# Up projection of a decoder layer: the low halves of three right operands are computed on GpSimd at the change of span

## The reference, cut to what matters

```python
h = rmsnorm(x, norm_ffn_pre[l])
up = causal_depthwise_conv(h @ w_up[l], conv_w[l], conv_b[l])   # w_up: 1024 x 5632
gate, val = up[..., :D_FF], up[..., D_FF:]                       # D_FF = 2816
f = (jax.nn.silu(gate) * val) @ w_down[l]
x = x + rmsnorm(f, norm_ffn_post[l])

def causal_depthwise_conv(h, conv_w, conv_b):                    # CONV_WIDTH = 3
    S = h.shape[1]
    hp = jnp.pad(h, ((0, 0), (CONV_WIDTH - 1, 0), (0, 0)))
    y = conv_b
    for kk in range(CONV_WIDTH):
        y = y + conv_w[kk] * hp[:, kk:kk + S]
    return y
```

## Time and profile before

| | us |
|---|---|
| median of 3 runs | 2625.34 (2622.07 to 2629.64) |
| the profiled execution: its own time | 2622.72 |
| its span in the trace | 2621.0 |
| PE busy in the span | 2432.5 (93%) |
| DVE busy in the span | 1653.4 (63%) |
| POOL busy in the span | 737.3 (28%) |
| the up projection in the span | about 1214 to 2092 |
| the stretch of the change of span | about 1640 to 1692 |

### The profile page before, as it was taken

One profiled execution on the slowest core, in us unless ns is written; L12 is line 12 of the kernel. 1 busy time (PEld: TensorE's weight loads), 2 busy tenths in 40 slices (PEclk: granted clock), 3 DMA queues, 4 the chain that ended last, 5 costly groups with the idle time before them and its releaser, 6 DMA issues. The chain is left out here.

```text
span 2621.0 us, 38066 instructions
## 1 busy us (share of the span) xinstructions
PE 2432.5 (93%) x11925; PEld 2000.5 (76%) x11925; DVE 1653.4 (63%) x2099; ACT 1230.4 (47%) x2065; POOL 737.3 (28%) x624
## 2 busy tenths in 40 slices
PE   6989996999999979994999999799999899999997
PEld 5767885878788868883888888688888778778785
DVE  4424222999898977874877777877777734443433
ACT  4311112888888864554444444444444423242322
POOL 0000001686666643554222222222222000110101
PEclk9989997999999989996999999899999999999999
DMA  7922435243333215676232222523222154545452
GB/s 240 286 65 80 132 122 148 57 123 91 86 89 86 73 54 162 217 241 192 73 94 74 86 82 76 181 72 96 72 88 80 65 188 145 188 148 192 148 189 107
DMA packets 283122, 326.90 MB, mean 125 GB/s; under 512 B 11972, under 2 KB 217468, under 8 KB 278396
## 3 DMA queue, kind: packets, MB, share of 16 engines
q1 hardware_dynamic: 278396, 308.68, 38.5%
q0 software_dynamic: 4608, 16.78, 1.6%
HBM read 216.36 MB, written 92.27 MB: 118 GB/s over the span
## 5 line engine op out<-in xcount | busy, mean ns | idle before, releaser
L740 POOL TENSOR_TENSOR weight<-beta,stick 128x512 f32<-128x512 f32 (+3 forms) x320 | 304.4, 958 | 601.8 <-ACT beta L694 449.9
L786 DVE TENSOR_TENSOR_SCAN stick<-z_ps,stick,beta 128x512 f32<-128x512 f32 x192 | 245.2, 1277 | 25.2 <-ACT z_ps L695 24.2
L511 PE MATMUL out_ps<-hT,w_hi 128*128 128x512 f32 x768 | 240.4, 395 | 9.8 <-DVE w_lo L445 9.8
L1629 PE MATMUL value_chain_ps<-wide,wu_hi 128*128 128x512 f32 x704 | 220.2, 394 | 16.4 <-DVE up_cols L1578 9.7
L694 ACT ACTIVATE beta<-z_ps 128x512 f32<-128x512 f32 (+3 forms) x320 | 170.7, 533 | 92.1 <-PE z_ps L820 78.5
L1409 ACT ACTIVATE wu_hi<-wu_sums 128x512 fp32r<-128x512 f32 x175 | 110.4, 632 | 187.3 <-PE value_chain_ps L1629 93.0
L837 PE MATMUL wT_ps<-ident,weight 128*128 128x128 f32 x1088 | 174.0, 275 | 11.0 <-POOL weight L740 11.0
L1746 POOL TENSOR_TENSOR y<-y,x 128x1024 f32<-128x1024 f32 x16 | 38.9, 2432 | 504.8 <-DVE y L1805 504.6
L511 PEld LDWEIGHTS out_ps<-hT,w_hi 128*128 128x128 f32 x768 | 145.5, 190 | 42.2 <-DVE w_lo L445 10.2
L695 ACT ACTIVATE z_ps<-z_ps 128x512 f32<-128x512 f32 (+3 forms) x320 | 171.5, 536 | 0.0
L1629 PEld LDWEIGHTS value_chain_ps<-wide,wu_hi 128*128 128x128 f32 x704 | 134.0, 191 | 45.6 <-DVE wu_lo L1506 10.0
(11 more groups left out here) (209 smaller groups left out, 6232.2 us busy)
## 6 DMA issues: line engine op xcount, KB each, us to landing
wu_f<-in_w_down SPq DMA_DIRECT2D x88, 512.0 KB, 3.5
wu_f<-in_w_up SPq DMA_DIRECT2D x44, 512.0 KB, 5.0
bridge<-in_w_up SPq DMA_DIRECT2D x44, 512.0 KB, 5.0
f_scratch<-f SPq DMA_DIRECT2D x44, 512.0 KB, 2.6
wu_sums<-f_scratch SPq DMA_DIRECT2D x88, 256.0 KB, 3.7
x_scratch<-x SPq DMA_DIRECT2D x56, 256.0 KB, 2.6
xt<-in_x SPq DMA_DIRECT2D x16, 512.0 KB, 5.7
hT<-h_hi SPq DMA_DIRECT2D x16, 512.0 KB, 4.7
```

What stands on the lines that cost most here:

```text
L511: m = pe.matmul(out_ps[half + j][:, :], w[slot][:, k, :], hT[h][:, k, j * BANK:(j + 1) * BANK], start=(k == 0 and t == 0), stop=(k == kc - ...
L740: pool.tensor_tensor(weight[v % weight_ring][:, 0:w], beta[v % stick_in][:, 0:w], stick[q % 2][:, at:at + w], ALU.mult).then_inc(weight_do ...
L786: dve.tensor_tensor_scan(stick[q % 2][:, at:at + w][:, ::-1], backwards, beta[u % stick_in][:, 0:w], start, ALU.mult, ALU.bypass).then_inc ...
L1629: m = pe.matmul(bank[:, :], w[left][:, k, :], x[right][:, k, :], start=(not adds and k == 0 and t == 0), stop=(k == half - 1 and t == 2), ...
```

## The change

At the change of span, the low halves of right operands 2, 4 and 6 are computed on GpSimd (`by_pool`), those of 0, 1, 3 and 5 still on VectorE. In the first span nothing is changed. The three have a semaphore of their own, `x_pool_done`, and TensorE's wait in `ready` looks at the one or the other.

```diff
+        x_pool_done = n.sem("x_pool_done")
+        by_pool = (2, 4, 6)
@@ GpSimd
+                def right_low(part, operand):
+                    pool.wait_ge(x_hi_done, 7 * part + operand)
+                    pool.tensor_tensor(x_lo[operand], as_f32(x_lo[operand]), as_f32(x_hi[operand]), ALU.subtract).then_inc(x_pool_done, 1)
+
                 def unit(u, part, j, e, pair):
                     if not is_last(u):
                         left_sums(u + 1, 1 - e, pair + e)
+                    if at_part_end(u, part):
+                        right_low(part + 1, 2)
+                        right_low(part + 1, 4)
+                    if past_part_end(u, part):
+                        right_low(part, 6)
@@ VectorE
                 def right_low(part, operand):
+                    if part > 0 and operand in by_pool:
+                        return
                     dve.wait_ge(x_hi_done, 7 * part + operand)
@@ TensorE
                 def ready(u, operand, part):
                     i = UP_LEFT.index(operand)
                     pe.wait_ge(wu_done, split_of(u, operand))
-                    pe.wait_ge(x_done, 7 * part + i + 1)
+                    if part == 0:
+                        pe.wait_ge(x_done, i + 1)
+                    elif i in by_pool:
+                        pe.wait_ge(x_pool_done, len(by_pool) * (part - 1) + by_pool.index(i) + 1)
+                    else:
+                        pe.wait_ge(x_done, 7 + (7 - len(by_pool)) * (part - 1) + sum(1 for k in range(i + 1) if k not in by_pool))
```

## The result

| | before | changed |
|---|---|---|
| median of 8 runs, us | 2625.76 (2622.07 to 2629.68) | 2632.53 (2630.18 to 2633.80) |
| ratio of the times, 95% interval | | 1.0024 (1.0013 to 1.0035) |
| span of the profiled execution, us | 2621.0 | 2630.3 |

The changed kernel is slower by 6.3 us by the ratio, with an interval of 3.4 to 9.2 us. The ratio lies within 0.3%, but its interval reaches to 0.35%. The forecast was 2633 us and +7.8 us, in the range of 2627 to 2639.

A forecast was written before the change was run, and what follows sets the result against it. TensorE bounds the kernel overall, but VectorE sets the pace at the change of span. Terms -6.6, +13.1, +3.3, -0.9, -0.6 and -0.5 sum to +7.8 us, on the median 2625.34 giving 2633 us, range 2627 to 2639.

The forecast's parts named there:

- TensorE hangs on line 1578 at the end of VectorE's queue: At the change of span, TensorE's 9.7 us wait is for line 1578 of unit 22, last in VectorE's queue.
- A GpSimd instruction costs VectorE its duration less 0.19 us: Where VectorE reads two SBUF tiles, GpSimd blocks it; three right operands come back as +13.1 us.
- GpSimd's 128x2048 takes 4.55 us: Time of each right operand's subtraction on GpSimd, taken from shorter ones, with bounds of 4.5 and 4.8 us.
- Three more sums, +3.3 us, less 0.6 us beside line 1524: Unit 23's sums fall later into VectorE's queue, three more at 1.10 us; one beside line 1524 doesn't block, -0.6 us.
- Gate taps earlier, -0.9 us: Two sums of unit 23 no longer block VectorE ahead of the gate taps, which end at 1658.8, not 1659.70.
- The idle time covered, -0.5 us: VectorE's idle 0.52 us at 1669.92, ahead of line 1578, is covered.
- The sum: Start of line 1578 of unit 22: +7.8 us, including -6.6 us for three right operands leaving VectorE.
- The same loss after the restart: After the long wait TensorE runs at about half clock for some us as before; nothing was put for it.
- New waits for operands 2 and 3 cost nothing: TensorE waits about 1.5 us and 4 us for them, swallowed by the long wait, which begins later.
- The first, GpSimd beside VectorE: GpSimd doesn't hold VectorE up over such a long instruction: -6.9 us, 2618.4 us; chance 6%.
- The second, VectorE winning turns: VectorE sometimes goes ahead though GpSimd asked first; operand 6 falls behind line 1578: +3.4 us, 2628.7 us; chance 9%.
- The third, a higher price: GpSimd takes 4.8 us or more each, full-length lock, longer low clock: +9 to +12 us, about 2636; chance 15%.

The follow-up runs named there:

- experiment 5: Kernel before, no GpSimd operands; in unit 22 lines 1535 and 1578 come right behind the split of a22: ratio 0.9981 (0.9972 to 0.9991).
- Experiment 3: The change, but GpSimd fills the low halves of operands 2, 4 and 6 with zero, reading nothing: ratio to before 0.9988 (0.9979 to 0.9997).
- Experiment 4: The change, but GpSimd makes the sums of unit 23 ahead of operands 2, 4 and 6: ratio to before 1.0015 (1.0006 to 1.0024).
- Experiment 2: The change with only operands 2 and 4 on GpSimd, operand 6 back on VectorE: ratio to before 1.0019 (1.0011 to 1.0028).
- experiment 6: The whole change plus lines 1535 and 1578 of unit 22 right behind the split of a22: ratio to before 1.0016 (1.0007 to 1.0025).
- experiment 7: Kernel before with lines 1535 and 1578 early in unit 22 and only operands 2 and 4 on GpSimd: ratio 1.0010 (1.0001 to 1.0019).
- experiment 8: Kernel before, no GpSimd operands; lines 1535 and 1578, then operand 5, ahead of unit 22's value taps: ratio 0.9992 (0.9983 to 1.0001).
- experiment 10: The whole change with each 128x2048 subtraction on GpSimd cut in four of 128x512: ratio to before 1.0019 (1.0010 to 1.0028).
- experiment 9: Kernel before, no GpSimd operands; lines 1535, 1578 and operand 5 early, line 1597 of unit 22 right behind operand 6: ratio 0.9991 (0.9982 to 1.0000).

## Why the prediction was right, point by point

- **TensorE hangs on line 1578 at the end of VectorE's queue.** Shown: the wait is for this line in the changed kernel too, and experiment 5, which moves only this line and the one it needs, takes D down by 5.1 us.
- **A GpSimd instruction costs VectorE its duration less 0.19 us.** Shown by the trace after: 5.08 - 0.68, 6.66 - 2.29 and 4.45 - 0.16 make 13.06 us of blocked time for the three. The term was +13.1. The Trainium skill ("SBUF — State Buffer", section "SBUF: two separate sides") has the lock for the whole instruction, and the trace agrees up to the 0.2 us of hand-over. Experiment 3 shows that it is the reading that matters.
- **GpSimd's 128x2048 takes 4.55 us.** No row has one that ran free. Behind VectorE's release at 1660.12 operand 2 took 4.45 us. In the rows of before a sum that stood waiting takes 0.14 us less behind VectorE's release than its 1.29 us, so by an estimate operand 2 alone would take 4.59 us. The Trainium skill's 4497 ns ("GPSIMD Engine Reference", section 3.1) is near it too.
- **Three more sums, +3.3 us, less 0.6 us beside line 1524.** Together +2.7. The rows give 0.36 us at the copy, 1.70 at the value taps and 1.10 at operand 5, 3.16 us for all four, where one with 1.10 was before: +2.06. Some of it fell while VectorE waited for ScalarE's value tap. Experiment 4 has 2.2 us for the place of the sums.
- **Gate taps earlier, -0.9 us.** They end 9.76 us after the start of operand 0 and not 10.55: -0.8.
- **The idle time covered, -0.5 us.** It is 0.16 and not 0.52 us: -0.4.
- **The sum.** -6.6 + 13.06 + 2.06 - 0.8 - 0.4 = +7.3 us, and D has +7.38. The forecast was +7.8, and most of the 0.4 us are those of the sums (+2.7 forecast, +2.06 read). The measured time, +6.3 us with an interval of 3.4 to 9.2, agrees but is too coarse to weigh single terms.
- **The same loss after the restart.** From TensorE's restart to the end of U it is 35.37 us and was 35.78, so 0.4 us came back. I had put nothing. The first product behind the restart takes 5.25 us at a granted clock of 0.53, and before it took 5.26 us at 0.50.
- **New waits for operands 2 and 3 cost nothing.** 1.55 and 4.12 us against 1.5 and 4 in the forecast. Experiment 2 has both of them, and its D is what the blocked time alone makes.
- **The rivals.** The first, GpSimd beside VectorE, is what experiment 3 looks like, and only without reads. The second, VectorE winning turns, was not seen in the change: GpSimd's next instruction begins its work at the first end of a VectorE instruction each time. But four other runs have one such turn each (last section), so it is not ruled out for another order. The third, a higher price, did not come: 4.59 us and not 4.8 for an instruction, and no more time at the low clock.
- **What was luck.** The forecast lay on the line of 0.3%, with the two sides given 0.46 and 0.48. On which side the ratio fell says nothing for the mechanism.

## What to carry to other kernels

Before work is moved from VectorE to GpSimd, look at what VectorE does meanwhile: against instructions with two SBUF inputs, and even against a copy of four columns, a 128x2048 subtraction on GpSimd cost 4.3 to 4.4 us to save 2.2. In the rows here GpSimd's work was free only beside instructions that read PSUM (0.68 us at 1671.62) and while VectorE stood idle (experiments 6 and 7); neither was tried with a whole 128x2048. First ask which single step the waiting engine hangs on, and whether it stands at the end of a queue for no reason: moving one line and its input gave 5 us here. A shorter wait at one step is not a shorter kernel, as D and U of experiments 8 and 10 show, so a second distance to the point where all is regular again belongs beside it.

## What the runs showed of the hardware

- A fill on GpSimd (128x2048, 1.81 us) doesn't stop VectorE's two-input subtraction (0.68 and 0.69 us inside of two fills). A `TENSOR_SCALAR` of 128x8 beside the third fill had a long row, 0.77 us for 0.16, that ended at 1678.62 with the fill that ends at 1678.59. Nothing behind it was held up.
- An engine that stands waiting mostly has the next turn. Two value taps in a row on VectorE let operands 4 and 6 through one after the other, 11.13 us for 2.60 (experiment 4). But it isn't strict. In experiments 5, 6, 7 and 9 the sum s1(24) was issued 0.23 us after the start of a split of 0.68 us, and VectorE's next split still went ahead of it and kept its 0.68 or 0.69 us. In experiment 8, with the same 0.23 us, the sum had the turn and the split took 1.75 us. What decides it is open. The rows of experiment 5, and then of experiment 8:

```profile
1684.87 0.69 DVE L1506 TENSOR_TENSOR wu_lo<-bridge,wu_hi 128x512 fp32r<-128x512 f32 x1
1685.10 2.21 POOL L1382 TENSOR_TENSOR wu_sums<-wu_f 128x512 f32<-128x512 f32 x1 [14.49 <-DVE wu_lo L1506]
1685.47 0.69 DVE L1506 TENSOR_TENSOR wu_lo<-wu_sums,wu_hi 128x512 fp32r<-128x512 f32 x1
```

```profile
1682.17 0.68 DVE L1508 TENSOR_TENSOR wu_lo<-bridge,wu_hi 128x512 fp32r<-128x512 f32 x1
1682.40 1.57 POOL L1382 TENSOR_TENSOR wu_sums<-wu_f 128x512 f32<-128x512 f32 x1 [14.75 <-DVE wu_lo L1508]
1682.77 1.75 DVE L1508 TENSOR_TENSOR wu_lo<-wu_sums,wu_hi 128x512 fp32r<-128x512 f32 x1
```
